# Query and key sums of squares in two rounded passes, with their stages placed anew, in a two-layer hybrid encoder

## What is computed

```
h = rms_norm(x, norm_w)
proj = h @ w_in                        # 5824 columns, shared out among four branches
A: differential attention, 4 heads     B: grouped-query attention, 4 heads, 2 key heads
C: latent attention, 4 heads           D: multi-scale pooling mixer
y = concat(each branch * silu(its gate))
x = x + y @ w_out
```

```python
def rms_norm(x, w):
    x32 = x.astype(jnp.float32)
    y = x32 * lax.rsqrt(jnp.mean(x32 * x32, axis=-1, keepdims=True) + EPS)
    return (y * w.astype(jnp.float32)).astype(x.dtype)
```

## Time and profile before

| | |
|---|---|
| time, median of 3 runs | 913.06 us (913.02 to 913.20) |
| the profiled execution | 912.77 us, of which its span is 911.0 us |
| TensorE busy | 899.7 us, 99% of the span |
| VectorE busy | 637.0 us, 70% |
| ScalarE busy | 585.5 us, 64% |
| granted TensorE clock | 1.00 of full speed throughout |
| mean rate of the transfers | 158 GB/s |

### The profile page before, as it was taken

How to read it: one execution, slowest core, us unless ns; L and a number is a source line. 1 busy time by engine, 2 the same in 40 slices (tenths; PEclk the granted TensorE clock), 3 DMA queues, 4 the chain that set the end, 5 groups by cost and what they waited for, 6 DMA issues and landing times.

```text
span 911.0 us, 18111 instructions
## 1 busy us (share of the span) xinstructions
PE 899.7 (99%) x7054; PEld 858.4 (94%) x7054; DVE 637.0 (70%) x1071; ACT 585.5 (64%) x1045; POOL 0.2 (0%) x4
## 2 busy tenths in 40 slices
PE   8999999999999999999999999999999999999998
PEld 7998998999999999999999989999999999999998
DVE  7785887768777776766665658876687667666552
ACT  7678756678666667745554588566686666675331
POOL 0000000000000000000000000000000000000000
PEclk9999999999999999999999999999999999999999
DMA  8654343343444343445455544334425344445562
GB/s 332 260 188 142 134 142 132 109 139 129 140 141 142 138 148 128 145 149 192 166 195 185 186 155 169 119 119 161 158 93 186 128 151 145 149 171 185 187 201 78
DMA packets 22997, 143.83 MB, mean 158 GB/s; under 512 B 2560, under 2 KB 4736, under 8 KB 6528
## 3 DMA queue, kind: packets, MB, share of 16 engines
q1 hardware_dynamic: 22768, 142.64, 44.0%
q10 hardware_dynamic: 144, 0.04, 0.0%
HBM read 140.57 MB, written 2.10 MB: 157 GB/s over the span
## 4 chain that ended last, share of the span: by engine, by line
PE 89%; ACT 7%; DVE 2%; issue 1%; DMA 1%; SPq 0%; ACTq 0%; DVEq 0%
PE dense L725 25%; PE dense L727 24%; PE dense L726 24%; PE s_ps L889 4%; PE o_ps L924 4%; ACT w_hi L1014 2%; PE norm_ps L845 2%; PE t_ps L905 2%; DVE w_lo L1319 1%; ACT qw L1087 1%; DMA x<-xt_dram 1%; PE swap_ps L860 0%; ACT sq L1084 0%; PE norm_ps L727 0%; PE swap_ps L727 0%
## 5 line engine op out<-in xcount | busy, mean ns | idle before, releaser
L725 PE MATMUL dense<-h_hi,w_hi 128*128 128x272 f32 (+2 forms) x1440 | 427.1, 297 | 1.5 <-DVE h_lo L1299 0.9
L727 PE MATMUL dense<-h_hi,w_lo 128*128 128x272 f32 (+2 forms) x1440 | 412.6, 287 | 0.0
L726 PE MATMUL dense<-h_lo,w_hi 128*128 128x272 f32 (+2 forms) x1440 | 410.6, 285 | 0.0
L1319 DVE TENSOR_TENSOR w_lo<-raw,w_hi 128x1024 fp32r<-128x1024 f32 (+1 forms) x257 | 313.3, 1219 | 88.4 <-ACT w_hi L1014 82.3
L1014 ACT ACTIVATE w_hi<-raw 128x1024 fp32r<-128x1024 f32 (+1 forms) x257 | 271.3, 1056 | 68.7 <-PE dense L727 53.9
L725 PEld LDWEIGHTS dense<-h_hi,w_hi 128*128 128x128 f32 x1440 | 271.3, 188 | 8.2 <-issue 3.8
L726 PEld LDWEIGHTS dense<-h_lo,w_hi 128*128 128x128 f32 x1440 | 271.5, 189 | 1.3
L727 PEld LDWEIGHTS dense<-h_hi,w_lo 128*128 128x128 f32 x1440 | 271.1, 188 | 0.0
L725 PE MATMUL dense<-y_hi,w_hi 128*128 128x272 f32 (+1 forms) x500 | 143.1, 286 | 2.3 <-ACT q_st L1059 1.3
L727 PE MATMUL dense<-y_hi,w_lo 128*128 128x272 f32 (+1 forms) x500 | 142.7, 285 | 0.0
L726 PE MATMUL dense<-y_lo,w_hi 128*128 128x272 f32 (+1 forms) x500 | 142.4, 285 | 0.0
(11 more groups left out here) (161 smaller groups left out, 813.4 us busy)
## 6 DMA issues: line engine op xcount, KB each, us to landing
raw<-w_stream_dram SPq DMA_DIRECT2D x128, 1024.0 KB, 4.8
out_dram<-x SPq DMA_DIRECT2D x8, 256.0 KB, 6.3
x<-xt_dram SPq DMA_DIRECT2D x3, 544.0 KB, 8.9
raw<-w_stream_dram SPq DMA_DIRECT2D x3, 512.0 KB, 7.5
con<-consts_dram SPq DMA_DIRECT2D x1, 984.0 KB, 7.4
x<-xt_dram SPq DMA_DIRECT2D x2, 272.0 KB, 4.8
raw<-w_stream_dram SPq DMA_DIRECT2D x2, 256.0 KB, 4.6
d_w<-consts_dram SPq DMA_DIRECT2D x2, 256.0 KB, 5.1
```

The source lines that it names most:

```text
L725: nc.tensor.matmul(ps, whi, xhi, start=first, stop=False)
L726: nc.tensor.matmul(ps, whi, xlo, start=False, stop=False)
L727: return nc.tensor.matmul(ps, wlo, xhi, start=False, stop=last)
L1319: signal(nc.vector.tensor_tensor(w_lo[:, g % RING, 0:n], raw[:, e % RAW, CHUNK * half:CHUNK * half + n], w_hi[:, g % RING, 0:n].bitcast(F3 ...
```

## The change

Four things are changed together.

1. **Sums.** The 36 sums of queries and keys are now two passes of the rounded type: squares `sq` = `sq_hi` + `sq_lo`, each multiplied with a rounded copy of the table (`sums_of`, made once in `lam_exp`). For unpaired ones ScalarE makes `sq_hi` (in `rope_pre`), for paired ones VectorE does (in `sq_sum`, behind the addition); VectorE subtracts to get `sq_lo` in either case (`sq_low` or `sq_sum`). The sums of the latents, of A's outputs and of x stay as they are.
2. **Bank.** `norm_free` waits for `norm_taken`, which the logarithm raises, and no longer for the exponential behind it.
3. **Up-projections.** `up_out` lifts one tile at a time. For the first three chunks the second tile's lift (`up_next`, 0.715) stands behind the split. Chunk 18's split is moved to nearly a slot earlier.
4. **Places.** `rope_pre` goes to 0.62, behind lifts and `p_out`; the squares' sum and low half to 0.64; `rope_mid` to 0.8, behind the split; ScalarE's `rope_fin` to -0.39 of the slot after the sum's, which is behind the lifts of the sum's own slot and ahead of its split. The sums of aq, ak and kr, and all that follows, come one slot later.

Small tiles are packed into `stat` and `v_st` to make room for the new ones; this adds no instruction.

```diff
-AT_SCALAR = dict(rope_fin=-0.166, ..., rope_pre=0.11,
+AT_SCALAR = dict(rope_fin=-0.39, ..., rope_pre=0.62,
...
-AT_VECTOR = dict(sq_sum=0.2, rope_mid=0.25, ...
+AT_VECTOR = dict(sq_sum=0.64, sq_low=0.64, lat_sum=0.2, rope_mid=0.8, ...
...
-MOVED = {**{("lift", l, 3, 0): -0.55 for l in range(DEPTH)},
+MOVED = {**{("lift", l, 3, 0): -0.55 for l in range(DEPTH)}, **{("split", l, 18): -0.98 for l in range(DEPTH)},
...
                     at(s, ("rope_pre", l, kind, i0 + j, j))
-                    at(s, ("rope_stat", l, kind, i0 + j))
-                    at(s + 1, ("rope_fin", l, kind, i0 + j))
+                    at(s, ("sq_low", "rope", l, kind, i0 + j))
+                    at(s + 1, ("rope_stat", l, kind, i0 + j))
+                    at(s + 2, ("rope_fin", l, kind, i0 + j))
...
         for c in range(U_CHUNKS):
-            at(s + 4 + c, ("up_out", l, c))
+            for j in range(UP_TILES[c]):
+                at(s + 4 + c, ("up_next" if c < 3 and j else "up_out", l, c, j))
...
+        def two(ps, table, hi, lo):
+
+            nc.tensor.matmul(ps, table, hi, start=True, stop=False)
+            return nc.tensor.matmul(ps, table, lo, start=False, stop=True)
+
         def norm_free(*stage):
             n = norm_order[stage]
             if n:
-                pe.wait_ge(rn_ready, n)
+                pe.wait_ge(norm_taken, n)
...
-            if key in PAIRED:
-                pe.wait_ge(summed, sum_no[("rope", l, key, i)])
-            else:
-                pe.wait_ge(pre_done, pre_no[("rope_pre", l, key, i)])
+            pe.wait_ge(summed, sum_no[("rope", l, key, i)])
             norm_free("rope_stat", l, key, i)
-            sums = nc.tensor.matmul(norm_ps[:, t0:L], halves, sq[:, 2 * parity("rope_stat", l, key, i), t0:L],
-                                    start=True, stop=True)
+            half = parity("rope_stat", l, key, i)
+            if (l, key, i) == (0, "kr", 0):
+                pe.wait_ge(ones_ready, 1)
+            sums = two(norm_ps[:, t0:L], halves_r, sq_hi[:, half, t0:L], sq_lo[:, half, t0:L])
...
-            square = nc.scalar.activation(sq[:, 2 * half, t0:L], src, ACT.Square)
-            if branch:
-                link(square)
-                square = nc.scalar.activation(qw[:, half, t0:L], src, ACT.Copy, scale=pcol(l, key))
-            signal(square, pre_done, pre_no[("rope_pre", l, key, i)])
+            link(nc.scalar.activation(sq[:, 2 * half, t0:L], src, ACT.Square))
+            link(nc.scalar.activation(qw[:, half, t0:L], src, ACT.Copy, scale=pcol(l, key)))
+            signal(nc.scalar.activation(sq_hi[:, half, t0:L], sq[:, 2 * half, t0:L], ACT.Copy),
+                   pre_done, pre_no[("rope_pre", l, key, i)])
...
-            link(nc.scalar.activation(rn[:, t0:L], norm_ps[:, t0:L], ACT.Ln, scale=1.0 / width, bias=eps_c[:, 0:1]))
+            signal(nc.scalar.activation(rn[:, t0:L], norm_ps[:, t0:L], ACT.Ln, scale=1.0 / width, bias=eps_c[:, 0:1]),
+                   norm_taken, n + 1)
...
-            signal(nc.vector.tensor_tensor(a, a, b, ALU.add), summed, n)
+            link(nc.vector.tensor_tensor(a, a, b, ALU.add))
+            high = sq_hi[:, half, t0:L]
+            link(nc.vector.tensor_copy(high, a))
+            signal(nc.vector.tensor_tensor(sq_lo[:, half, t0:L], a, high.bitcast(F32), ALU.subtract), summed, n)
```

More of the change, by code:

```diff
@@ L289, in build @@
     sq = sb("sq", [128, 4, L])
+    sums_of = sb("sums_of", [128, 256], F32R)
+    sq_hi = sb("sq_hi", [128, 2, L], F32R)
+    sq_lo = sb("sq_lo", [128, 2, L], F32R)
     qw = sb("qw", [128, 2, L])
@@ L303, in build @@
     lam_in = v_st[:, 0, 0:DEPTH * 256]
[L304 to L308 removed]
+    lam_sum = v_st[:, 1, 0:DEPTH * 2]
+    neg_lam, eps_c, one_c = stat[:, 2:2 + DEPTH], stat[:, 6:7], stat[:, 7:8]
     dense = [bank("dense0"), bank("dense1")]
@@ L318, in build @@
     ident, ones, halves = const("ident", 128), const("ones", 128), const("halves", 128)
+    ones_r, halves_r = sums_of[:, 0:128], sums_of[:, 128:256]
     def pcol(l, name, i=0):
@@ L914, in pv @@
             if branch == "c":
-                pe.wait_ge(up_taken, UP_TILES * (l + 1))
+                pe.wait_ge(up_taken, sum(UP_TILES) * (l + 1))
             else:
@@ L985, in lambda_exp @@
             signal(nc.scalar.activation(lam_sum[:, :], lam_sum[:, :], ACT.Exp), lam_exp, 1)
+            act.wait_ge(s_const, 16)
+            nc.scalar.activation(sums_of[:, :], con[:, CC["ones"]:CC["ones"] + 256], ACT.Copy).then_inc(ones_ready, 1)
         def x_tile(l, kt):
@@ L1344, in sq_sum, with sq_low @@
             a, b = sq[:, 2 * half, t0:L], sq[:, 2 * half + 1, t0:L]
-            signal(nc.vector.tensor_tensor(a, a, b, ALU.add), summed, n)
+            link(nc.vector.tensor_tensor(a, a, b, ALU.add))
+            high = sq_hi[:, half, t0:L]
+            link(nc.vector.tensor_copy(high, a))
+            signal(nc.vector.tensor_tensor(sq_lo[:, half, t0:L], a, high.bitcast(F32), ALU.subtract), summed, n)
+        def sq_low(what, *of):
+            stage = ("rope_stat" if what == "rope" else "sub_stat", *of)
+            l = of[0]
+            t0 = rope_from(l, of[1]) if what == "rope" else first_query(l)
+            dve.wait_ge(pre_done, pre_no[(("rope_pre" if what == "rope" else "sub_pre"), *of)])
+            half = parity(*stage)
+            signal(nc.vector.tensor_tensor(sq_lo[:, half, t0:L], sq[:, 2 * half, t0:L],
+                                           sq_hi[:, half, t0:L].bitcast(F32), ALU.subtract), summed,
+                   sum_no[(what, *of)])
         def rope_mid(l, key, i):
```

93 lines of the change are left out of this document (45 added, 48 removed).

## The result

The changed kernel takes **935.85 us** (934.68 to 936.78 in four runs) where the kernel before takes 913.04 beside it: a ratio of 1.0249 (95% interval 1.0231 to 1.0267). I had forecast 905.0 and 87% for "faster". It is 22.8 us slower, the side to which I had given 0.06.

A forecast was written before the change was run, and what follows sets the result against it. TensorE's stream of passes was taken as the bound (busy 899.7 of 911.0 us). Gains of 5.5 (sums after chunk 28), 0.7 (up to chunk 28) and 1.7 (single waits), about 8.0, took 913.06 to 905.0 us; 8-in-10 range 899.5 to 910.

The forecast's parts named there:

- The passes themselves: Sums on TensorE: two rounded passes, priced as dense ones, replace each float32 sum; gain 7.1 us over 36 sums.
- rival (c): Sums on TensorE: two passes no shorter than one float32 sum; 910.5 or 912.5 us; chance 0.07, shared with other no-change ways.
- The single lifts: Up-projections, chunks 16 to 20: lifting tiles singly removes standing still of 2.25 and 2.35 us; gain up to 4.6 us.
- Chunks 22 to 28: Latent stretch of each layer: VectorE's fuller queue takes back the earlier gains there, leaving 0.7 us over both layers.
- The walk: Hand-followed order of operations, chunks 22 to 28: TensorE waits 2 us at kn0's sum, 0.5 at qr0's; 25.1 us from chunk 21.
- no new stall outside chunks 22 to 28: All other stretches: the added steps and new places were given no cost in the sum.
- Rival (b): Other stretches with softmax and sums together also run out of VectorE room, taking 4 us: 909 us; chance 0.20.
- a gain of 1.7 us: Single waits of TensorE: squares moved behind the p_t copies and sums a slot behind squares remove waits, 1.7 us.
- over the whole run that is hidden: Added steps: ScalarE's 9.5 us and VectorE's 20 us fit into 325 and 274 us in which they don't work.
- Rival (d): Slower: every sum waits for a VectorE instruction; 919.5 us if on average 0.55 us late; chance 0.06.
- The two prices of nothing: Earlier release of the bank, and inverse roots ahead of the split on ScalarE: each priced at no gain or cost.

The follow-up runs named there:

- e4: Changed kernel with ScalarE's squares at 0.605 of a slot instead of 0.62, ahead of the logarithm: 920.55 us, ratio 1.0082.
- e7: Changed kernel with float32 sums and ScalarE's squares at 0.605 instead of 0.62, ahead of the logarithm: 909.61 us, ratio 0.9961.
- e3: Kernel before, with only the up-projections lifted singly and chunk 18's split earlier: 911.11 us, ratio 0.9979.
- e5: Two-pass kernel at the old places (928.46 us), but with float32 sums; added steps run on constants and nobody waits for them: 919.61 us, ratio 1.0072.
- e9: e4's kernel with the 36 subtractions and 14 rounding copies of paired sums moved from VectorE to GpSimd: 920.18 us, ratio 1.0078.
- e15: e4's kernel with only kn's four sums and roots one chunk later, steps on VectorE: 921.34 us, ratio 1.0090.
- e11: e4's kernel with all 36 sums and their roots one further chunk later, steps on VectorE: 921.57 us, ratio 1.0096.
- e12: e9's kernel (steps on GpSimd) with all 36 sums and their roots one further chunk later: 919.55 us, ratio 1.0073.
- e16: e9's kernel (steps on GpSimd) with only kn's four sums and roots one chunk later: 919.01 us, ratio 1.0065.
- e13: Changed kernel with norm_free waiting for rn_ready again, as before the change: 933.8 to 935.1 us, ratio 1.0233.
- e14: e7's kernel with the inverse roots back at -0.166, behind the split of the stream: 909.86 us, ratio 0.9966.
- e1: Changed kernel with its sums made again by one float32 matmul, all else of the change kept: 917.57 us, ratio 1.0050.

## Why the prediction was wrong

**The passes themselves: right.** They start 0.12 to 0.13 us apart where dense passes stand around them and nothing is late. Behind a wait or behind float32 score products the first takes 0.23 us, but the first half of a float32 sum took 0.33 behind such products where it took 0.23 otherwise, so the saving is the same 0.2; rival (c) is out. The steps' durations (means of one, changed kernel) are as priced: subtraction 443 ns, rounding copy on VectorE 302. ScalarE's rounding copy takes 431, as I had counted it there. The Trainium skill's page "VectorE: DVE Perf Modes" (The perf-mode tier table) puts a float32 copy at twice the rate of a two-operand instruction. The rounding copy agrees, which no row of before could show. The whole durations, 302 and 443 ns, aren't one to two, but the part that grows with the columns is: with 256 columns in place of 272 the copy takes 293 to 295 ns and the subtraction 426, so 8 and 17 ns less. The rows:

```profile
L1370 DVE TENSOR_TENSOR sq_lo<-sq,sq_hi 128x272 fp32r<-128x272 f32 x16 | 7.1, 443 | 15.0 <-ACT sq_hi L1099 14.9
L1360 DVE CAST sq_hi<-sq 128x272 fp32r<-128x272 f32 x10 | 3.0, 302 | 0.3
```

```profile
L1099 ACT ACTIVATE sq_hi<-sq 128x272 fp32r<-128x272 f32 x16 | 6.9, 431 | 0.5
```

**The single lifts: right in kind, two thirds in size.** Chunk 21 starts at 73.27 (I had 72.7), 1.65 us earlier than in the earlier trace rows; in layer 1 the stretch gains 1.44 of 2.35. No wait for `q_st` or `k_st` is left.

**Chunks 22 to 28: right mechanism, too small.** The walk said 2 us at kn0's sum and 0.5 at qr0's; TensorE shows

```profile
88.39 0.40 PE L829 MATMUL norm_ps<-sq_hi,sums_of 128*128 128x272 f32 x1 [1.99 <-DVE sq_lo L1361]
92.56 0.39 PE L829 MATMUL norm_ps<-sq_hi,sums_of 128*128 128x272 f32 x1 [0.62 <-DVE sq_lo L1370]
99.04 0.39 PE L732 MATMUL dense<-h_hi,w_hi 128*128 128x272 f32 x1
```

and chunk 28 at 99.04 against 97.8, 0.96 later than in the earlier trace rows instead of 0.3 earlier. From chunk 21 to 28 that is 25.8 us where the walk had 25.1; the other 0.6 is the lifts. The walk stopped at chunk 28. Its next station was kn1's sum at 114.81, in the same state with more softmax in VectorE's queue: it waited 2.2 us in each layer. Had I walked on to chunk 33, the stretch would have cost more than both parts gained.

**The first step that failed: no new stall outside chunks 22 to 28.** My sum has no cost for the other stretches, since I took from shares of busy time that TensorE waits for VectorE only where VectorE is full. Rival (b) had such a cost, 4 us with a chance of 0.20. Chunks 33 to 62 are less full, and they lost 13.6 us, with only one wait for `sq_lo` (1.7 us, layer 1) among them. There the new place of the squares did it: with the squares first (e4) the same chunks lose -0.72 + 1.11 + 0.14 + 1.17 = 1.7 us. The prediction had seen the move "from ahead of the `p_t` copies to behind them" and booked it as a gain of 1.7 us. It never asked what the squares had moved behind besides: the logarithm, which itself waits for TensorE's last sum (38.0 us in all) and for VectorE's use of the last root (20.0). **Of a moved step I counted what it passes, not what the instruction ahead of it waits for.** With the squares at 0.605 a gain of that size may be there: e7 is 1.5 us under e3, within their intervals.

**The second, and the larger: the cost of the steps, "over the whole run that is hidden".** This was false in both kernels with two passes: 18.0 us with squares first (10.9 + 7.1), 25.4 with the loop (18.3 + 7.1), against 5.5 in my sum (6.2 of gain in the latent stretches, of which 0.7 was left). e5 shows that 6.5 us come even if nobody waits for the steps. Some 3 us are the clock. e9 and e15 show that neither another engine nor more lead for the latest sums takes the rest away: each returns it at another place (e11 and e12 say so less cleanly, as 4 us of theirs are a side effect). I can't split it further: in e16, at full clock, 9.4 us over the float32 kernel remain, 6.9 of its waits at GpSimd's subtraction and the rest in waits of at most 1.8 us.

**Rival (d) had the side right, and its mechanism in part.** 913.06 - 13.4 + 36 x d = 935.85 gives d = 1.0 us per sum, where I had tried 0.55, with 0.06 as its chance. But TensorE waited for VectorE at 8 sums, for 11.8 us, or 0.33 a sum; the rest is the loop, the softmax and the others behind the fuller queues. With the squares first the same sum gives d = 0.58. My argument against (d) was that before no chunk waited for its `w_lo`. That said that VectorE had been in time for steps with several chunks of lead. A sum of squares has one.

**The two prices of nothing held** (e13, e14). The change of 22.8 us comes apart, by the runs, into lifts and places with squares first -3.4 (e7), squares behind the logarithm +8.0 (e1), two passes +18.3. These are differences along one way from before to after, so that they add up proves nothing; with the passes first and the order last it is -3.4, +10.9 and +15.3.

## What to carry to other kernels

A faster instruction on the bound engine is paid for in the chain that feeds it: count the hand-overs between engines from its input to its start (here squares, rounding, subtraction) and compare them with the lead in the order, not with the idle share of the engines. More lead isn't free either: here it moved the lateness to the next customers (e15). Before moving a step in a queue, list what the instruction that will stand ahead of it waits for; if that depends on the step's own customers, the move closes a loop. Here 0.015 of a slot cost 8 to 15 us. And if the accuracy allows it, drop the work that needs the hand-over rather than hide it: one rounded pass gave 5.9 us, and two exact ones lost 10.9.
